# Two transformer blocks in one kernel: middle layer re-ordered around its attention, depthwise convolution in 32x32 products, and x split before it is scaled

## What is computed

```python
# first block, layer 0
p = rmsnorm(x, g_mix[0]) @ w_in_a            # 2*768 + 256 columns
a, gate = split(p[:, :1536] + b_glu)
v = a * sigmoid(gate)
v = causal_dwconv(v, w_dw_a, b_dw_a)         # 31 taps per channel, 768 channels
mix = silu(layernorm(v, ln_g, ln_b))
# first block, layer 1 (the middle layer)
kvf = rmsnorm(x, g_kv) @ w_kvf               # keys, values, forget gates of 12 heads
p = rmsnorm(x, g_mix[1]) @ w_in_b            # 768 + 256 query columns
mix = forgetting_attention(q, k, v, cum_logf)        # causal, 12 heads of 64
# both layers
mem_o = memory_attention(q_mem, mem_k, mem_v)        # 4 heads over 256 memory rows
x = x + concat(mix, mem_o) @ w_out
x = x + conv_ffn(rmsnorm(x, g_ffn), w_up, w_dw_f, b_dw_f, w_down)
# second block, twice
h = rmsnorm(x) ; gated MLP over tokens, grouped attention with 8 heads, w_out, rmsnorm, add
```

## Time and profile before

| | |
|---|---|
| median of three runs | 1854.2 us (1853.27 to 1857.57) |
| the profiled execution, its own time | 1855.58 us |
| its span, first to last instruction | 1853.8 us |
| busy in it: TensorE, weight loads | 92%, 71% |
| VectorE, ScalarE, GpSimd | 49%, 40%, 40% |
| mean granted TensorE clock | 0.965 of 2.4 GHz |

### The profile page before, as it was taken

One profiled execution on the slowest core, in us unless ns is written; L12 is line 12 of the kernel. 1 busy time (PEld: TensorE's weight loads), 2 busy tenths in 40 slices (PEclk: granted clock), 3 DMA queues, 4 the chain that ended last, 5 costly groups with the idle time before them and its releaser, 6 DMA issues.

```text
span 1853.8 us, 22551 instructions
## 1 busy us (share of the span) xinstructions
PE 1701.9 (92%) x7866; PEld 1307.3 (71%) x7866; DVE 912.0 (49%) x1405; ACT 748.0 (40%) x1186; POOL 741.5 (40%) x403
## 2 busy tenths in 40 slices
PE   4968889999999999888999999999799998899995
PEld 3645667888888877644778888888576666676674
DVE  5999535455530032344266666400656354746444
ACT  4233444444432223255255555422426542427440
POOL 2454533444444433433434444444224433333430
PEclk9989889999999999998999999999899998999997
DMA  4110312233233322200223322333221113111111
GB/s 172 60 51 27 103 57 80 91 102 101 91 102 109 106 91 80 80 12 1 69 71 102 100 91 94 116 107 102 86 69 46 57 46 97 66 49 57 46 45 46
DMA packets 39380, 142.59 MB, mean 77 GB/s; under 512 B 4368, under 2 KB 4368, under 8 KB 38928
## 3 DMA queue, kind: packets, MB, share of 16 engines
q1 hardware_dynamic: 38592, 139.57, 23.2%
q10 hardware_dynamic: 720, 2.10, 0.3%
HBM read 139.55 MB, written 2.10 MB: 76 GB/s over the span
## 4 chain that ended last, share of the span: by engine, by line
PE 75%; issue 9%; DVE 8%; ACT 4%; POOL 4%; POOLq 0%; DVEq 0%; ACTq 0%
PE banks L1278 22%; PE banks L1279 21%; PE banks L1280 21%; POOL w_lo L465 3%; PE banks L1416 3%; PE banks L1399 2%; PE banks L1379 2%; ACT prob L568 1%; PE banks L1357 1%; DVE sq_sum L846 1%; DVE pt L1265 1%; DVE nmax L908 1%; DVE xs_lo L1135 1%; PE banks L1552 1%; PE banks L1563 1%
## 5 line engine op out<-in xcount | busy, mean ns | idle before, releaser
L465 POOL TENSOR_TENSOR w_lo<-raw,w_hi 128x1024 fp32r<-128x1024 f32 x255 | 656.8, 2586 | 904.9 <-ACT w_hi L520 904.9
L1278 PE MATMUL banks<-xs_hi,w_hi 128*128 128x512 f32 x1592 | 643.5, 404 | 43.9 <-DVE xs_lo L1135 12.8
L1280 PE MATMUL banks<-xs_hi,w_lo 128*128 128x512 f32 x1592 | 626.8, 394 | 0.0
L1279 PE MATMUL banks<-xs_lo,w_hi 128*128 128x512 f32 x1592 | 626.7, 394 | 0.0
L1278 PEld LDWEIGHTS banks<-xs_hi,w_hi 128*128 128x128 f32 x1592 | 303.4, 191 | 128.3 <-issue 53.8
L520 ACT ACTIVATE w_hi<-raw 128x1024 fp32r<-128x1024 f32 x255 | 263.2, 1050 | 283.2 <-PE banks L1280 277.5
L1280 PEld LDWEIGHTS banks<-xs_hi,w_lo 128*128 128x128 f32 x1592 | 302.7, 190 | 64.8
L1279 PEld LDWEIGHTS banks<-xs_lo,w_hi 128*128 128x128 f32 x1592 | 303.8, 191 | 62.1 <-issue 2.9
L475 POOL TENSOR_SCALAR prob<-prob,rinv 128x512 f32<-128x512 f32 (+3 forms) x144 | 84.6, 600 | 168.1 <-DVE rinv L917 168.1
L1278 PE MATMUL banks<-hid_hi,w_hi 128*128 128x512 f32 x352 | 136.9, 389 | 0.0
L1279 PE MATMUL banks<-hid_lo,w_hi 128*128 128x512 f32 x352 | 136.9, 389 | 0.0
(11 more groups left out here) (193 smaller groups left out, 1749.6 us busy)
## 6 DMA issues: line engine op xcount, KB each, us to landing
raw<-wstream SPq DMA_DIRECT2D x255, 512.0 KB, 3.4
x<-xT SPq DMA_DIRECT2D x2, 1024.0 KB, 6.3
out<-x SPq DMA_DIRECT2D x8, 256.0 KB, 2.0
memx<-memT SPq DMA_DIRECT2D x1, 1024.0 KB, 11.2
ws_sb<-wsT ACTq DMA_DIRECT2D x2, 512.0 KB, 3.8
sb_sb<-sbT ACTq DMA_DIRECT2D x2, 256.0 KB, 4.2
rope_sb<-rope ACTq DMA_DIRECT2D x1, 512.0 KB, 5.0
par<-params SPq DMA_DIRECT2D x1, 338.5 KB, 2.9
```

Source lines behind the costliest of these rows:

```text
L465: nc.gpsimd.tensor_tensor(w_lo[s][:].rearrange("p k c -> p (k c)"), raw[s][:], w_hi[s][:].rearrange("p k c -> p (k c)").bitcast(f32), SUB) ...
L1278: MM(dst, w_hi[slot][:, k, :], hi, start=start, stop=False)
L1279: MM(dst, w_hi[slot][:, k, :], lo, start=False, stop=False)
L1280: return MM(dst, w_lo[slot][:, k, :], hi, start=False, stop=stop)
```

## The change

It has four parts.

1. *x is split as it comes*, in four transfers, with the gain only; the inverse root is multiplied in when a unit leaves PSUM (`glu_half`, on VectorE instead of ScalarE; `mem_down` for the memory units). The first unit does not wait for the squares.
2. *The convolution* has 16 taps on TensorE and 15 on VectorE. The diagonal weights become 32x32 blocks, made by GpSimd. Row group i of 32 channels writes to its own bank, and column group j holds the sum of every fourth tap; ScalarE copies the four banks out, and four products with `fold` add the column groups.
3. *The middle layer* has the queries first, then gates, keys and values in turn. The steps of both attentions are placed between passes by `B_AT`; `xs_hi` is rewritten for the keys pass by pass as the last query unit releases it (`xs_free`), and again for the outputs. The attentions use the `spaced` banks, two sets of transposed tiles in turn, and leave their outputs in SBUF (`o_down`).
4. The second block's three attention calls are the same ones, split into `scores`, `output`, `transposes`; the first two output units of the middle layer run together.

```diff
-PE_TAPS = 8
+Q = 32
+NQ = P // Q
+PE_TAPS = 16
+QM_UNIT, Q_UNIT, F_UNIT = 0, 2, 2 + MT
+K_UNIT = (9, 10, 12, 14, 16, 18)
+V_UNIT = (11, 13, 15, 17, 19, 20)
+B_AT = [(3 + i, 4) for i in range(8)]
+B_AT += [divmod(11 * KT + 40 * p // 3 + q, KT) for p in range(MT) for q in (0, 3, 6, 10)]
+B_LATE = 7
...
# POOL
-            lows(0, U_OUT0 + AHEAD)
+            for t in range(MT):
+                low((2 * t) % SLOTS, 2 * t)
+                low((2 * t + 1) % SLOTS, 2 * t + 1)
+                if t >= 2:
+                    pool.wait_ge(part_up, NQ * (t - 1))
+                nc.gpsimd.tensor_tensor(diag[t % 2][:], fold.unsqueeze(1).to_broadcast([P, PE_TAPS, Q]),
+                                        par[:, w0:w0 + PE_TAPS].unsqueeze(2).to_broadcast([P, PE_TAPS, Q]),
+                                        MUL).then_inc(diag_ok, 1)
+            lows(2 * MT, U_OUT0 + AHEAD)
             scale_probs(att_m0)
-            lows(U_OUT0 + AHEAD, U_OUT1 + AHEAD)
-            scale_probs(att_f)
-            scale_probs(att_m1)
+            lows(U_OUT0 + AHEAD, U_B + AHEAD)
+            for j in range(B_UNITS):
+                low((U_B + j + AHEAD) % SLOTS, U_B + j + AHEAD)
+                for k in range(KT):
+                    for i in b_steps(j, k):
+                        scale_block(*b_block(i))
...
# ACT
-                act.wait_ge(unit_used, 2 * t + 1)
-                A(glu[:, t, CW - 1:], acc[0][:], ACT.Identity, bias=col("b_glu", t)).then_inc(acc_free, 1)
-                for tap in range(PE_TAPS):
-                    ins = A(diag[:, tap, :], ident, ACT.Copy, scale=col("w_dw_a", t * CW + DVE_TAPS + tap))
-                act.wait_ge(unit_used, 2 * t + 2)
-                A(gate[t % 2][:], acc[1][:], ACT.Sigmoid, bias=col("b_glu", MT + t)).then_inc(acc_free, 1)
+                if t:
+                    parts_down(t - 1)
+                act.wait_ge(acc_free, 2 * t + 2)
+                A(gate[t % 2][:], gate[t % 2][:], ACT.Sigmoid, bias=col("b_glu", MT + t)).then_inc(gate_ok, 1)
...
# DVE
+            def glu_half(t, e):
+                if t < MT:
+                    scaled(glu[:, t, CW - 1:] if e == 0 else gate[t % 2][:], 2 * t + e)
+                else:
+                    scaled(qm0[:, e, :], U_QM0 + e, factor=HD ** -0.5)
...
+                    if tap == 5:
+                        glu_half(t + 1, 0)
+                    if tap == 12:
+                        glu_half(t + 1, 1)
...
# PE
+            def conv_parts(t):
+                pe.wait_ge(glu_ok, t + 1)
+                pe.wait_ge(diag_ok, t + 1)
+                if t:
+                    pe.wait_ge(part_down, NQ * t)
+                for g in range(PE_TAPS // NQ):
+                    for j in range(NQ):
+                        tap = g * NQ + j
+                        for i in range(NQ):
+                            rows = slice(Q * i, Q * (i + 1))
+                            last = MM(b_part[i][Q * j:Q * (j + 1), :], diag[t % 2][rows, tap, :],
+                                      glu[rows, t, DVE_TAPS + tap:DVE_TAPS + tap + T], start=g == 0,
+                                      stop=g == PE_TAPS // NQ - 1)
+            def conv_fold(t):
+                pe.wait_ge(part_down, NQ * (t + 1))
+                for i in range(NQ):
+                    MM(b_fold[Q * i:Q * (i + 1), :], fold, part[i][:], start=True, stop=True).then_inc(fold_up, 1)
...
-            attend(att_f)
-            attend(att_m1)
+            def b_step(i):
+                if i < B_BLOCKS:
+                    a, n = b_block(i)
+                    if a is att_f and n == 0:
+                        pe.wait_ge(f_done, 2)
+                    scores(a, n)
+                late = b_pair(i)
+                if late is not None and late != (att_f, MT - 2):
+                    b_output(*late)
+                if i:
+                    transposes(*b_block(i - 1))
```

More of the change, by code:

```diff
@@ L97 @@
 N_PARAMS = _place_params()
[L98 removed]
+N_CONSTS = 4 * P + 2 + N_FOX + Q
 class Tally:
@@ L211, in two_blocks @@
         vm0 = take("vm0", [P, 2, TM])
+        pt0_at = take.at()
         pt0 = [take(f"pt0_{i}", [P, 2, T]) for i in range(2)]
+        part = [put(f"part{i}", [P, T], f32, pt0_at + i * T * 4) for i in range(NQ)]
         sqm = [take(f"sqm{i}", [P, TM]) for i in range(2)]
@@ L1307, in two_units @@
                 for k in range(KT):
+                    for at, step in before:
+                        if at == k:
+                            step()
                     pe.wait_ge(split_lo, first + k + 1)
@@ new lines, in transposes @@
+            def transposes(a, i):
+                b = a.i0 + i
+                for e in range(2):
+                    pe.wait_ge(at_p, 2 * b + e + 1)
+                    if b:
+                        pe.wait_ge(at_pt_odd if e else at_pt_even, b)
+                    for k in range(keys_of(a, i % QT) // P):
+                        last = nc.tensor.transpose(a.t[e][:, k * P:(k + 1) * P],
+                                                   prob[b % 2][:, e, k * P:(k + 1) * P], ident)
+                    last.then_inc(at_t, 1)
@@ new lines, in output @@
+            def output(a, p):
+                n = a.p0 + p
+                pe.wait_ge(at_pt_even, a.i0 + QT * (p + 1))
+                pe.wait_ge(at_pt_odd, a.i0 + QT * (p + 1))
+                n1 = n - len(a.o)
+                if n1 >= 0:
+                    b = [c for c in attentions if c.p0 <= n1][-1]
+                    s, v = b.read(n1 - b.p0)
+                    pe.wait_ge(s, v)
+                nt = a.keys // P
+                for k in range(nt):
+                    q0 = k * P if a.causal else 0
+                    for e in range(2):
+                        last = MM(a.o[n % len(a.o)][half(e), q0:T], a.v_of(2 * p + e, k), pt_of(a, p)[e][:, k, q0:T],
+                                  start=(k == 0), stop=(k == nt - 1))
+                        if k == nt - 1:
+                            last.then_inc(at_o, 1)
```

535 lines of the change are left out of this document (300 added, 235 removed).

## The result

The changed kernel takes **1805.62 us** (median of 4 runs, 1805.25 to 1806.57), the kernel before 1854.18: a ratio of 0.9736, 95% interval 0.9719 to 0.9753. The forecast was 1804, range 1780 to 1828. The profiled execution of the kernel after has a span of 1804.8 us and its own time is 1806.57, so 49.0 us of span are gone; the sum said 49.9.

What follows compares the result with a forecast made beforehand. VectorE was taken to bound the convolution, and no engine to be full in the middle layer's attention. Gains of 5.5 + 20 + 24.4 = 49.9 us, and 1.4 for the median, took 1855.6 to 1804 us, range 1780 to 1828.

Steps and rivals of the forecast that it cites:

- Part 1, the start: Start up to the first gated tile: root applied after the units, first gated tile near 40 us, 5.5 us earlier.
- Part 2, the convolution: Convolution stage: taps moved from VectorE to TensorE shorten it from 146.1 to 125.7 us, 20 us less.
- Taps, -32: Convolution on VectorE: 8 of 23 taps per channel tile leave, 32 us less over six tiles.
- Twelve releases, +7.7: Convolution on VectorE: 12 releases of units taken over from ScalarE add 7.7 us, at 0.69 each less the overlap.
- Small products, 3.4 to 6.9 us per tile: Convolution on TensorE: 64 products of 32x32 per tile take 3.4 us if sixteen sub-arrays run together, up to 6.9.
- Part 3, the middle layer: Middle layer, first unit's first product to first output unit's: 229.7 us falls to 205.3, 24.4 us less.
- New waits: Middle layer: queries to keys 1.5, gates' chain 3, late blocks 4, last pair 2; 10.5 us in the sum.
- A forgetting pair: Middle layer: each of six pairs of forgetting heads takes 9.7 us without its idle times, 58.1 in all.
- B: Convolution's small products four abreast, only row or only column groups overlapping: 13.7 us per tile, 1850 us; chance 0.05.
- C: Convolution's small products only two abreast: 27.4 us per tile, kernel slower than before at 1932 us; chance 0.03.
- D: Middle layer's blocks come back late, GpSimd scaling them behind low weights: layer gains 5 us, kernel 1823; chance 0.09.
- E: Convolution stage keeps its length because GpSimd, locked out during taps, delays weights: kernel 1825 us; chance 0.05.

Runs made afterwards that it cites:

- experiment 9: Changed kernel with the column sums of squares of x before the first unit instead of behind the second unit's fourth pass: 1803.34 us.
- experiment 10: Changed kernel with the hidden tiles' base 128 bytes higher and the column sums of squares of x right behind the first unit: 1792.94 us.
- experiment 12: Kernel of experiment 10 with the six diagonal tiles made by ScalarE (16 copies each) instead of one GpSimd operation each: 1789.22 us.
- experiments 1 to 3: Hidden tiles' base moved: changed kernel at 137600, 1795.95 us; kernel before at 137728, 1861.23 us; changed kernel at 137856, 1797.72 us (single run).
- Experiments 5 and 6: Changed kernel, 64 small products reordered: row group by row group, 1830.41 us; each four in a row on the same sub-array, 2100.12 us (single run).
- experiment 6: Changed kernel with each four small products in a row on the same 32 by 32 sub-array: 2100.12 us (single run).

## Why the prediction was right, step by step

**Part 1, the start: near enough.** glu at 38.16 instead of near 40, 7.25 us earlier, not 5.5. The first unit ended at 21.4 (21 forecast), the second started at 22.65 (23), the sums came at 25.51 (27), the root at 33.2 (34). The sum gave TensorE's early first product no value of its own, and experiment 9 bears that out: 10 us later, the kernel is no slower. That the root's chain keeps its old length of 7 us came out, but the sum didn't say why it is that long: GpSimd holds it up, and moving it forward doesn't shorten the start by as much (experiment 10).

**Part 2, the convolution: total right, terms wrong by as much as they cancel.** From the first glu to the channel sum's product 127.65 us (125.7 forecast), ending at 165.81 (166). Groups of VectorE by line over the stage, the taps of before and then taps and additions of after:

```profile
L1048 DVE SCALAR_TENSOR_TENSOR chain<-glu,par,chain 128x512 f32<-128x512 f32 x126 | 84.0, 744 | 0.0
L1022 DVE TENSOR_TENSOR conv<-conv,chain 128x512 f32<-128x512 f32 x6 | 10.5, 1743 | 0.0
L1023 DVE TENSOR_TENSOR conv<-conv,chain 128x512 f32<-128x512 f32 x6 | 8.3, 1376 | 0.2
```

```profile
L1125 DVE SCALAR_TENSOR_TENSOR chain<-glu,par,chain 128x512 f32<-128x512 f32 x78 | 68.5, 938 | 0.0
L1092 DVE TENSOR_TENSOR conv<-conv,chain 128x512 f32<-128x512 f32 x6 | 8.4, 1396 | 0.2
...
L1089 DVE SCALAR_TENSOR_TENSOR conv<-banks,par,chain 128x512 f32<-128x512 f32 x6 | 4.5, 745 | 0.0
```

- *Taps, -32:* only -15.5. 48 taps left, but each of the 78 that stay keeps VectorE 0.88 us instead of 0.67, 16.5 us in all. Before, GpSimd waited for the taps (12.07 us for one operation, mean 4.96 in the stage); after, it takes 2.66 on average and the taps wait. I had charged for six diagonal tiles, 5 us, and not for the stage's 13 low-weight operations, some of which now get in too. Here is one that does, on GpSimd and then on VectorE:

```profile
105.13 2.48 POOL L503 TENSOR_TENSOR w_lo<-raw,w_hi 128x1024 fp32r<-128x1024 f32 x1 [1.66 <-ACT w_hi L573]
```

```profile
105.27 0.68 DVE L900 TENSOR_TENSOR glu<-banks,rstd 128x512 f32<-128x512 f32 x1
105.87 6.26 DVE L1125 SCALAR_TENSOR_TENSOR chain<-glu,par,chain 128x512 f32<-128x512 f32 x7
```

It starts just ahead of a release, which reads PSUM and keeps its 0.68 us; the seven taps behind it need 6.26 instead of the 4.72 that they take where nothing is beside them. It looks as if the releases, now set between taps, open the gap through which GpSimd gets in. That fits the rows; no run took the releases out, so the cause is argued, the cost is measured.
- *Six diagonal tiles, +5:* experiment 12 prices them at 3.7 us of the kernel and 6.8 of the taps' busy time.
- *Additions and glu around the taps:* not in my sum, and they gave some 14 us back (18.8 to 12.9 in the rows above, the channel sums 9.6 to 3.5, glu 6.3 to 4.5): before, some of them were the ones that GpSimd hit (1743 ns on average where 0.69 us is the plain length). That is what cancelled the taps. VectorE's collisions moved; I had only counted new ones.
- *Twelve releases, +7.7:* 0.68 each, as charged. The rule of the Trainium skill (SBUF — State Buffer, Who interferes with whom) holds on them: 0.68 us beside a running GpSimd operation. The 7 us less that I read out of it didn't come: GpSimd does slip in under the releases, and the taps behind pay.
- *Small products, 3.4 to 6.9 us per tile:* 4.46 at full clock. The Trainium skill (TensorE: Matmul & The Clock Gate, Part 3: Packing small matmuls) has 10.6 times for sixteen tiles, from which I had an estimate of 5.2 us. Here it is about 12 times, against an estimate of 55 us for 128 instructions at the wide ones' 0.43 us; no run issued them singly at full clock, and why it is more than 10.6 was not tried. The 0.5 us for changes of mode is there: 16.75 less the small products (4.39 to the next start), the fold (1.00) and two units (10.88) leaves 0.48. "VectorE stays the bound" failed for the first two tiles, where TensorE is full at 16.7, and for the fifth, where it is full because it is cold. The other late tiles wait for VectorE, as forecast.
- *Cover after the last tile, nothing:* 27.0 us gained at the channel sum, 24.6 at the first attention. The cover cost 2.4.

**Part 3, the middle layer: mechanism right, too small by 10.0 us.** Forecast 277.3 - 24.4 = 252.9 us up to the second feed-forward, measured 242.9. Two terms hold it. *New waits* were charged at 10.5 and are 3.8: queries to keys 1.4 (1.5), gates' chain and late blocks together 1.3 (7), last pair 1.1 (2). *A forgetting pair* was charged at 9.7: from one pair's last scores (744.29) to the next one's (762.84) are 18.55 us, less 40 products (9.07) and a turned value group (0.6) 8.9, six times 0.8 less. Timeline of PE in the kernel after, one such pair:

```profile
744.29 1.13 PE L1518 MATMUL banks<-kf,qf 64*128 64x512 f32 x4
...
751.60 1.04 PE L1536 MATMUL banks<-cst,prob 128*128 128x128 f32 x8
753.18 0.60 PE L1506 MATMUL banks<-cst,vst 128*128 128x128 f32 x4
...
762.84 1.13 PE L1518 MATMUL banks<-kf,qf 64*128 64x512 f32 x4
```

These come to 11.6, and some 1.6 us went elsewhere. The first was plain caution, with bounds of 0 and 15 for the late blocks. The second is not a matter of the clock: the pair of the earlier trace rows, 805.46 to 816.75, ran at a granted clock of 1.00, though its stretch as a whole had 0.91. Why the same 69 instructions are 0.8 us shorter between passes was not worked out.

The round trip of a block was worked out well: that of 744.29 comes back from GpSimd at 750.29 (748.90 + 1.38), 4.4 us after its last score product, as forecast, and no transpose between passes waits for it.

**What the sum left out: "the long feed-forward stretches are untouched".** They were touched through the addresses: 7.0 us for both, experiments 1 to 3. A root's chain that meets one more GpSimd operation costs 1.7 us, and in the second block the clock is 0.96 instead of 0.97 for the same waits, some 2 us. Against part 3's 10 us to the good these weigh about as much, so two errors of some 10 us cancel: the forecast was right within its range, and luckier than its parts.

**The rivals.** B and C needed sub-arrays that queue: 4.46 us refutes both. Experiments 5 and 6 show something near them by the issue order: 9.16 us (B had 13.7), and two abreast as in C, 29 us by the estimate above (C had 27.4), 55.5 with the half clock. Both are summed half a microsecond per tile too low: part 2 has 12.3 us for units, fold and modes, the rivals 11.8. With 12.3 they give 1853 and 1935 instead of 1850 and 1932. D: no transpose between passes waited for GpSimd; two at the end did, 1.0 us in all. E: GpSimd was not locked out, it was VectorE that waited; part 2's gain is there.

## What to carry to other kernels

Put the blocks of a long round trip between passes of other work: here, with one score buffer, it was worth 37.8 us, of which 14.3 in the layer are busy time at a colder clock (236.2 to 250.5). Cost an edit on VectorE together with GpSimd: time that one of the two no longer loses to the other is often lost by the other instead, so sum both engines' busy time by line before and after. When a constant tile grows, look at the start of every tile behind it: compare the spacing of untouched products in the two traces. And before a measured time is taken as the proof of a price, look at the clock and at the single starts: 55.46 us was the number expected, and not the thing expected.

## What the runs showed of the hardware

- With the hidden tiles' base at 137728, 128x512 products that stream them start every 233.3 ns, at 137600 (either kernel) and 137856 (the changed one, a single run) every 226.7: 3% on 1056 products.
- 64 products of 32x32 by 512 columns: 4.46, 9.16 or 55.5 us by issue order, the last at half the clock; 32, 64 and 80 of them, packed, take 2.35, 4.46 and 5.53 us, about 1.1 us per round of sixteen.
- In experiment 6 TensorE was busy throughout with small products two abreast, and its granted clock was 0.50 from 47.7 us to 105.8; with the same products sixteen abreast it stayed at 1.00 (45.26 to 62.01).
- A VectorE operation on 4 columns (0.16 us) took 2.3 us beside a GpSimd operation, three times in one chain of twelve (experiment 10).
